# Two expert gates' weights ahead of their two ups' in a two-block kernel, and four idle matmuls fewer

## What is computed

```
def hier_moe(h, rg_w, rg_b, re_w, re_b, e_gate, e_up, e_down):
    ...
    for e in range(N_EXP):                       # 16 experts, 1024 x 512 and 512 x 1024
        he = jax.nn.silu(xt @ e_gate[e]) * (xt @ e_up[e])
        y = y + comb[:, e:e + 1] * (he @ e_down[e])
    return y.reshape(b_, s_, d_)

x = x + hier_moe(h2, ...)
x = rms_norm(x, norm_f_g)                        # end of the first block
h = rms_norm_2(x, norm1_g_2)                     # start of the second
p = h @ w_in_2
```

## Time and profile before

| | |
|---|---|
| median of 3 runs | 2055.51 us |
| lowest and highest | 2054.67 and 2059.64 us |
| the profiled execution | 2054.67 us |
| its span | 2053.2 us |
| PE busy | 1880.1 us, 92% of the span |
| DMA moved | 589.80 MB, mean 287 GB/s |
| mean granted clock of PE | 0.982 of full speed |

### The profile page before, as it was taken

The page is one execution under the profiler, slowest core; times in us unless marked ns, Lnnn a source line. Parts: engine busy times, 40 slices in busy tenths (PEclk is TensorE's granted clock), DMA queues, the critical chain, the costliest instruction groups (busy, mean ns, idle before and its releaser), DMA issues.

```text
span 2053.2 us, 19423 instructions
## 1 busy us (share of the span) xinstructions
PE 1880.1 (92%) x8428; PEld 766.4 (37%) x8428; DVE 491.8 (24%) x978; ACT 272.0 (13%) x478; POOL 32.6 (2%) x44
## 2 busy tenths in 40 slices
PE   8999999999999989899998999988788888888886
PEld 4444444453333335454445333322223222222222
DVE  3456000331101037980123011111101111110112
ACT  3322000121010125203111000000000000000001
POOL 0000000001000010000000000000000000000000
PEclk9999999999999999999999999999999999999999
DMA  6221032448999962112257999999999999999996
GB/s 238 82 82 41 0 123 82 181 152 329 405 410 390 400 222 83 42 41 77 82 218 286 410 428 427 428 428 427 428 428 428 428 428 427 428 428 427 427 428 272
DMA packets 68537, 589.80 MB, mean 287 GB/s; under 512 B 5472, under 2 KB 6880, under 8 KB 37216
## 3 DMA queue, kind: packets, MB, share of 16 engines
q1 hardware_dynamic: 59904, 556.55, 65.8%
q10 hardware_dynamic: 4448, 17.28, 2.1%
q0 software_dynamic: 4096, 14.68, 2.1%
HBM read 575.91 MB, written 12.58 MB: 287 GB/s over the span
## 4 chain that ended last, share of the span: by engine, by line
PE 61%; DMA 30%; DVE 7%; issue 2%; ACT 1%; POOL 0%; ACTq 0%; DVEq 0%
PE ps L251 23%; DMA ring<-in_w_up 21%; PE ps L1037 11%; PE ps L2184 8%; DMA ring<-in_w_down 7%; PE ps L2210 7%; PE ps L665 3%; PE ps L1827 3%; PE ps L265 2%; PE ps L587 1%; PE ps L1718 1%; PE ps L2165 1%; DMA ring<-in_exp_w_gate 1%; PE ps L280 0%; PE ps L1058 0%
## 5 line engine op out<-in xcount | busy, mean ns | idle before, releaser
L251 PE MATMUL ps<-AR,ring 128*128 128x512 f32 x1160 | 500.6, 592 | 3.9 <-DVE AR L2040 2.7
L251 PEld LDWEIGHTS ps<-AR,ring 128*128 128x128 f32 x1160 | 219.5, 190 | 277.8 <-issue 274.3
L2184 PE MATMUL ps<-AR 128*64 128x512 f32 x1040 | 236.7, 600 | 36.4 <-DMA AR<-in_w_up 25.1
L2322 DVE TENSOR_TENSOR XT<-XT,ps 128x512 f32<-128x512 f32 x128 | 82.0, 684 | 783.6 <-PE ps L2165 783.6
L2184 PE MATMUL ps<-ring,AR 128*64 128x512 f32 x1008 | 229.2, 598 | 39.4 <-DMA ring<-in_w_up 29.7
L1037 PE MATMUL ps<-ring,AR 128*32 128x512 f32 x1536 | 249.5, 597 | 3.3 <-ACT AR L1185 1.9
L2184 PEld LDWEIGHTS ps<-AR 128*64 128x64 f32 x1040 | 72.2, 137 | 193.1 <-issue 122.6
L2184 PEld LDWEIGHTS ps<-ring,AR 128*64 128x64 f32 x1008 | 67.9, 136 | 197.4 <-issue 116.8
L2210 PE MATMUL ps<-ring,AR 128*64 128x512 f32 x512 | 119.5, 611 | 8.5 <-DMA ring<-in_w_down 7.4
L1037 PE MATMUL ps<-AR 128*32 128x512 f32 x768 | 125.1, 595 | 0.0
L2210 PE MATMUL ps<-AR 128*64 128x512 f32 x512 | 120.8, 626 | 1.3 <-ACT AR L2247 1.3
(11 more groups left out here) (352 smaller groups left out, 1094.2 us busy)
## 6 DMA issues: line engine op xcount, KB each, us to landing
AR<-in_w_gate SPq DMA_DIRECT2D x33, 2048.0 KB, 33.6
ring<-in_w_up SPq DMA_DIRECT2D x32, 2048.0 KB, 35.4
AR<-in_w_up SPq DMA_DIRECT2D x32, 2048.0 KB, 33.6
ring<-in_w_down SPq DMA_DIRECT2D x32, 2048.0 KB, 35.4
AR<-in_w_down SPq DMA_DIRECT2D x32, 2048.0 KB, 35.4
ring<-in_w_gate SPq DMA_DIRECT2D x31, 2048.0 KB, 35.0
ring<-in_w_in SPq DMA_DIRECT2D x15, 2048.0 KB, 8.9
ring<-in_exp_w_gate SPq DMA_DIRECT2D x15, 2048.0 KB, 8.2
```

The source lines that it names most:

```text
L251: x = PE.matmul(ps, l, r, start=i == 0, stop=i == len(pairs) - 1)
L2184: x = PE.matmul(GU[2 * m + f // 2][64 * (f % 2):64 * (f % 2) + 64, :], XS[n // 2 % 2][:, k * P + 64 * b:k * P + 64 * b + 64], w[:, kk_, f ...
L2322: DV.tensor_tensor(XK[:, o:o + T], XK[:, o:o + T], co_bank(i)[:, :], ALU.add).then_inc(d_co, 1)
```

## The change

Within each pair of experts the load list takes gate, gate, up, up, where it took gate, up, gate, up. Since buffers go by place in the list, the second gate of a pair and the first up exchange their buffers. The two limits of the loops in `sp_front` and `sp_experts` are renamed so that the same number of loads (up to entry 18) is issued in the front, and the wait for `s_yp` and `s_ri` stands ahead of entry 16 as before. In the join, 8 idle products are issued for 12.

```
             if p < 8:
                 for e in (2 * p, 2 * p + 1):
                     load(f"eg{e}", runs(A["exp_w_gate"][e], 0, 8), fj_g, e + 1)
+                for e in (2 * p, 2 * p + 1):
                     load(f"eu{e}", runs(A["exp_w_up"][e], 0, 8), fj_u, e + 1)
...
-            for n in range(1, at["eu2"]):
-                if n == at["eg1"]:
+            for n in range(1, at["eg3"]):
+                if n == at["eu0"]:
                     SP.wait_ge(s_yp, 4)
                     SP.wait_ge(s_ri, 16)
                 sp_load(n)
...
         def sp_experts():
-            for n in range(at["eu2"], at["2pa"]):
+            for n in range(at["eg3"], at["2pa"]):
                 sp_load(n)
...
-            idle_products(bank[7], 12)
+            idle_products(bank[7], 8)
             turn(0)
```

## The result

The changed kernel took 2077.65 us (median of 4 runs, 2073.32 to 2078.42); the kernel before took 2055.09 us beside it. The ratio is 1.0103, with a 95% interval of 1.0081 to 1.0127: some 21 us slower (the two medians are 22.6 us apart). The prediction had the sign and said 2065 us with a range to 2073, so it was too low by more than half of the loss. The profiled execution took 2073.95 us (span 2072.6), 19.3 us above that of before. It is 3.7 us under the median, so that the trace accounts for 19 us of the loss and not for the last 2 or 3.

What follows compares the result with a forecast made beforehand. The prediction took PE to bound the first block's expert stage and transfers the second's. It added 8.4 us for the load order and 2.0 for fewer idle products, +10.4 on 2054.67, giving 2065 us, range 2058 to 2073.

Steps and rivals of the forecast that it cites:

- What bounds, and where a loss goes: First block's expert stage: PE sets the pace; a microsecond lost there reaches the end whole, the last stage absorbing none.
- Part 1: Expert stage's new load order: the second load waits for both_b, the last up lands third and late; +8.4 us.
- first term: Expert stage, pair 2: up_a(2) waits for its last up weights and starts 1.6 us late.
- a sign of being wrong: Expert stage: the prediction would be wrong if the waits for up weights grew from pair to pair.
- the forecast 8.4: Expert stage: delay of up_a(7)'s start from late last ups and a 36.15 us loop per pair; +8.4 us.
- It spreads: Rival, expert stage: new PE gaps may bring half clock, or the load queue backs up; 2077 us, chance 0.09.
- Part 2: Join before turn(0): 8 idle products for 12 leave PE idle about 4.1 us, half clock follows; +2.0 us.
- clock stays up: Rival, join: the clock does not fall, so fewer idle products cost nothing; 2063 us, chance 0.15.
- The third load was never in time: Judges a rival, expert stage: third load lands in time or nearly, 2056 to 2060 us, chance 0.14.
- Nothing was gained from the gates: Judges a rival, expert stage: earlier gate weights save PE waits, making it faster at 2054 us; chance 0.04.
- +20 for part 1: Expert stage, upper bound of the load order's cost: first landing at 10.4 us per group, loop 38.45 us; +20 us.

Runs made afterwards that it cites:

- e3: New load order with 12 idle products, second gate and first up swapping buffers in pairs 2, 4, 6 so the second load's buffer frees early; ratio 1.0015 to before.
- e7: Kernel before with its old load order, buffers swapped in pairs 2, 4, 6 so the second load waits for both_b of the previous pair; ratio 1.0159.
- e4: e1 plus two idle products ahead of the wait for up weights in up_a of pairs 2 to 7; ratio 1.0037 to before.
- e12: e4 run once more, unchanged; ratio 1.0051 to the kernel before.
- e1: Kernel before with only the new load order and its buffers, 12 idle products kept at the join; 2074.06 us, ratio 1.0085.
- e6: Kernel before with two idle products added ahead of the wait of down(7) and four ahead of that in states_rows; ratio 0.9997.
- e2: Kernel before with its old load order and only the join changed, 8 idle products for 12; 2059.99 us, ratio 1.0023.
- e5: Kernel before with its old load order and no idle products before turn(0), for 12; 2057.09 us, ratio 1.0010.
- e10: e4 with 8 idle products for 12 at the join, so the whole change with the six waits filled; ratio 1.0062 to before.

## Why the prediction was wrong

**What bounds, and where a loss goes: right.** The loss in the expert stage reached the end whole: the shift is 17.4 us at the end of down(6), 18.3 at v_part(0), and 19.4 at the end of the span. The last stage took nothing back.

**Part 1, the mechanism and its first term: right.** Six waits for the last up, the first of 1.56 us for 1.6 forecast; three loads at the end of both_b; third landing at 19.8 us for 19.7; the loop 36.2 and 36.5 us for 36.15 where the clock stayed up. The waits grew from 1.56 to 2.33 us, which the prediction had named as a sign of being wrong: the third load lands 20.6 us after the first of its group leaves in the last pair. Why it lands later there is not shown; it costs little over 1 us in all. e3 and e7 show that the wait, and not the order, is the cause. With the clock held (e4, e12) this is a loss of some 8 to 10 us by the medians, and of 8.6 to 9.5 us in the stage itself, for the forecast 8.4.

**The step that failed: the clock behind the six new waits was priced at nothing.** The prediction took 16.2 us from the start of up_a to the next group from a trace in which PE never stopped there, and put half clock behind the new idle times among the rivals, with 0.09 ("It spreads"). In the profile after, four of the six waits were followed by it, each time for 1.4 to 1.7 us: up_a(7) is 15.2 us late after the first 0.8, of which 1.5 + 5 x 36.3 - 174.0 = 9.0 is the loop at full clock, 5.0 the slower up_a of pairs 3, 4 and 6 (8.77, 8.68 and 8.77 us for 7.08), and the last 1.2 the later landings; pair 7 adds 1.4 of clock. A slower up_a also delays both_b and with it the next group, so that no later slack gives it back. e1 against the runs with the clock held shows the size: 1.0085 for 1.0037 (e4) and 1.0051 (e12), 7 to 10 us; in the profiles of the stage 10.5 to 11.5 us for e1 and 7 to 8 for the changed kernel. The trace of before had an instance of it in this very stage: PE idled 1.93 us ahead of down(7), with half clock behind it (mean 0.66 from 731.5 to 736.5, shown under e6). The prediction did not use it.

**Part 2: mechanism right, the term mis-sized.** 2.0 us was taken, with 3 as the upper bound; alone it measured 4.8 (2.7 to 6.8). In e2's profile the half clock reached into v_part, as the upper bound had it, and cost 3.5 us; in the profile after it ended with turn(0) and cost 1.4. The "clock stays up" rival is out: in each of the four profiles with a longer idle time there (after, e2, e5, e10: 3.55 to 10.03 us) turn(0) ran partly at half clock. The advice of the Trainium skill, "TensorE: Matmul & The Clock Gate", section "Why this matters for your kernels", not to leave TensorE idle between bursts, agrees with these runs.

**The other rivals.** The third load was never in time. The fit in the Trainium skill, "DMA: Bandwidth & Descriptors", section "Anatomy of one DMA", is stated for GpSimd-issued transfers only, and the 6.8 us estimated from it for 2 MB lies under what SP's loads took: 7.7 to 9.1 us for the first load of each group in the profile after. Nothing was gained from the gates, for there were only 0.6 us to gain. The range ended at 2073 because the upper bounds were weighed as unlikely each by itself, while the wait comes six times and the clock can fall at each. "It spreads" named the right mechanism and its 2077 lies at the measured median, but that agreement is luck: its +20 for part 1 was worked out from a first landing of 10.4 us in each group, which did not come (7.7 to 9.1), and holds nothing for the clock in the stage.

## What to carry to other kernels

A queue that issues in order turns a reorder of loads into a reorder of waits: before moving an entry, write down for each position which release it waits for and what stands behind it. A new wait on the engine that sets the pace has two prices, its length and the slower clock that may follow it, and the second enters every loop that the work behind the wait closes. Filling such a wait with idle products returned the second price only, as long as the products ended before the data landed and PE did not idle again right after. And where a stretch that no edit touches spreads by 5 us between executions, compare the stage of the edit by itself as well as the medians.

## What the runs showed of the hardware

Of the twelve waits of up_a in the profiles of after and e1, 1.38 to 3.13 us long, nine were followed by half clock. The length alone does not decide: 1.38 us was followed by it in e1, 1.40 us in the same profile and 1.56 and 1.71 us in that of after were not. The wait ahead of down(7), 1.82 to 2.11 us long in 13 profiles, was followed by half clock in ten (mean 0.72 to 0.74 over the next 6 us) and not in three (e1, e4 and e12, 1.00). In the last stage of the kernel before, some 80 waits for gate and up weights, up to 1.7 us long, were each followed by 16 instructions in 3.65 us, and the one of 2.74 us by 16 in 5.35 us. An idle time of 10 us before turn(0) cost less (1.4 us) than one of 4.2 (3.5): the clock came back within turn(0) in the one, and in v_part in the other. One stretch of 160 us with the same program took 158.4, 160.7 or 163.1 us at a mean clock of 0.97, 0.96 and 0.95: this alone is 0.2% of the kernel's time, about the size of the smaller effects measured here.
